# Layer 0's feed-forward stage in seven products per 128 hidden columns, and where the second layer's modulation is computed

## The reference, cut to what matters

```python
cond = jax.nn.silu(c)
for i in range(DEPTH):                       # DEPTH = 2
    mod = (cond @ ada_w[i] + ada_b[i])[:, None, :]
    sh1, sc1, g1, sh2, sc2, g2 = jnp.split(mod, 6, axis=-1)
    h = rmsnorm(x, norm_mix[i]) * (1 + sc1) + sh1
    ...                                      # i = 0: windowed attention, i = 1: dilated attention
    x = x + g1 * y
    h = rmsnorm(x, norm_ffn[i]) * (1 + sc2) + sh2
    x = x + g2 * swiglu(h, ffn_w_in[i], ffn_w_out[i])   # (silu(h@Wg) * (h@Wu)) @ Wo, 2816 hidden columns
```

## Time and profile before

| | us |
|---|---|
| median of 3 runs | 2860.38 (2860.36 to 2861.19) |
| time of the profiled execution | 2857.41 |
| its span in the profile | 2855.6 |
| PE busy | 2738.8 (96%) |
| DVE busy | 1662.7 (58%) |
| ACT busy | 887.2 (31%) |
| POOL busy | 273.4 (10%) |

### The profile page before, as it was taken

The page is one execution under the profiler, slowest core; times in us unless marked ns, Lnnn a source line. Parts: engine busy times, 40 slices in busy tenths (PEclk is TensorE's granted clock), DMA queues, the critical chain, the costliest instruction groups (busy, mean ns, idle before and its releaser), DMA issues. The chain is left out here.

```text
span 2855.6 us, 33976 instructions
## 1 busy us (share of the span) xinstructions
PE 2738.8 (96%) x13022; PEld 2161.8 (76%) x13022; DVE 1662.7 (58%) x2833; ACT 887.2 (31%) x1503; POOL 273.4 (10%) x425
## 2 busy tenths in 40 slices
PE   6999798999999999999998989999999999999798
PEld 5666487888888888876676677888888878879767
DVE  6777745444333334755656688777787785331653
ACT  5544513111111111344444153333333341101132
POOL 2110000000000001100000000000000039920000
PEclk9999899999999999999999899999999999979899
DMA  5223222222222221100011011111111131121212
GB/s 222 82 84 113 106 82 70 84 82 85 91 89 73 73 73 66 74 30 30 23 38 75 30 34 56 51 51 55 51 51 55 48 106 40 51 38 39 81 37 74
DMA packets 145817, 192.55 MB, mean 67 GB/s; under 512 B 6416, under 2 KB 114160, under 8 KB 145424
## 3 DMA queue, kind: packets, MB, share of 16 engines
q1 hardware_dynamic: 133232, 147.44, 15.5%
q0 software_dynamic: 12480, 43.68, 4.9%
HBM read 177.33 MB, written 12.58 MB: 67 GB/s over the span
## 5 line engine op out<-in xcount | busy, mean ns | idle before, releaser
L1101 PE MATMUL psum<-hT_high,w_low 128*128 128x512 f32 x1624 | 469.3, 392 | 2.1 <-DVE arena L2734 2.1
L1101 PEld LDWEIGHTS psum<-hT_high,w_low 128*128 128x128 f32 x1624 | 306.9, 189 | 67.1 <-DVE arena L2734 2.3
L2263 DVE SCALAR_TENSOR_TENSOR xT<-psum,mod,xT 128x1024 f32<-128x1024 f32 x176 | 223.1, 1279 | 72.4 <-PE psum L1385 72.4
L1101 PE MATMUL psum<-hT_high,w_high 128*128 128x512 f32 x744 | 230.3, 391 | 10.7 <-DVE w_low L2533 5.9
L1101 PE MATMUL psum<-h_low,w_high 128*128 128x512 f32 x736 | 227.5, 390 | 0.0
L1148 PE MATMUL psum<-hT_high,w_low 128*128 128x512 f32 x480 | 203.7, 424 | 2.5 <-DVE h_low_mix L2623 1.8
L1864 ACT ACTIVATE arena<-arena 128x384 f32<-128x384 f32 (+3 forms) x320 | 157.6, 494 | 117.1 <-DVE arena L2445 117.1
L1150 PE MATMUL psum<-hT_high,w_low 128*128 128x512 f32 x480 | 188.6, 393 | 0.0
L1149 PE MATMUL psum<-h_low_mix,w_low 128*128 128x512 f32 x480 | 187.7, 391 | 0.0
L2541 DVE TENSOR_TENSOR arena<-arena,psum 128x1024 f32<-128x1024 f32 x22 | 26.9, 1221 | 274.3 <-PE psum L1101 274.3
L1101 PE MATMUL psum<-hid_high,w_low 128*128 128x512 f32 x608 | 183.6, 391 | 0.8 <-DVE hid_low L2643 0.8
(11 more groups left out here) (352 smaller groups left out, 5262.1 us busy)
## 6 DMA issues: line engine op xcount, KB each, us to landing
arena<-in_ada_tiles_dram POOLq DMA_DIRECT2D x48, 512.0 KB, 3.6
wpair<-in_ffn_w_in_dram SPq DMA_DIRECT2D x22, 1024.0 KB, 5.1
wpair<-in_ffn_w_in_dram SPq DMA_DIRECT2D x88, 256.0 KB, 2.9
wpair<-in_ada_tiles_dram POOLq DMA_DIRECT2D x16, 1024.0 KB, 5.3
wpair<-in_w_in_dram SPq DMA_DIRECT2D x24, 512.0 KB, 3.8
wpair<-in_ffn_w_out_dram SPq DMA_DIRECT2D x11, 1024.0 KB, 4.8
wpair<-in_ffn_w_out_dram SPq DMA_DIRECT2D x44, 256.0 KB, 2.8
wpair<-in_b_tiles_dram SPq DMA_DIRECT2D x18, 512.0 KB, 3.3
```

What stands on the lines that cost most here:

```text
L1101: mm = nc.tensor.matmul(dst[:, HALF * t:HALF * t + HALF], w(k), src(k)[:, HALF * t:HALF * t + HALF], start=first and n == 0 and w is high ...
L2263: nc.vector.scalar_tensor_tensor(xT[:, m, :], acc[m % 2] if src is None else src, mod[:, l, 40 + m:41 + m], xT[:, m, :], ALU.mult, ALU.add ...
```

## The change

Layer 0's feed-forward stage is `feed(0, 0)`, the code that layer 1 used before (now `feed(1, 1)`), and `ffn` with its helpers is gone. `norm(1)` makes the first token differences as `norm(3)` does. The memory of the feed stage overlaps `cond`, so silu(c) is loaded and computed a second time (`cond_late`) in the attention of layer 1.

The second layer's 48 modulation tiles go elsewhere: 8 of them with layer 0's in `attention(0, 4)`, where a unit now has five pieces, in steps n = 0, 2, 4, 6 and 7; 8 stay in the `wo` stage (`second_piece`); 32 become `late_piece`, one tile per step in t = 36 to 67, from one landing buffer, issued by POOL when the tile before has been read. SP waits for `ada_read` 20 (16 before) ahead of layer 0's `wo` tiles, and for 60 ahead of layer 1's. In the last step of `feed(0, 0)` SP loads the first two tiles of the next attention, and the first is split there and not in `norm(2)`. POOL's distance and bias tables of layer 1 begin after the last product of the feed stage (before: after the last gate and up tile of `ffn`), and only two of its six bias tables are made ahead.

The diff, cut to its core (the text of the removed `ffn` functions is left out):

```diff
@@ plan_accumulators, plan_weights @@
-    use.block(("ffn", 0), ffn + [0], ffn_frees + [0])
+    use.block(("ffn", 0), [0] * 4, [0] * 4)
...
+    def second_mix(names):
+        for n, name in enumerate(names):
+            s.add(name, (1, 2)[n] if n < 2 else n % 2, name)
...
-    mix(MIX_TILES[1])
+    second_mix(MIX_TILES[1])
@@ buffers @@
+        ada_late, cond_late = wpair[2][:, 0:D], wpair[2][:, D:2 * D]
@@ SP @@
-            sp.wait_ge(ada_read, 16)
+            sp.wait_ge(ada_read, 20)
             for m in range(2, KC):
                 load_tile(("wo", 0, m), wo_rows[0][:, :, P * m:P * m + P], KC)
-            load_ffn(0)
-            load_mix("kv", 4)
+            load_steps(0, lambda n: load_mix(("kv", "q0")[n], 4))
...
+            sp.wait_ge(ada_read, 60)
             for n in range(3):
                 load_tile(("wo", 1, n), wo_rows[1][:, :, 256 * n:256 * n + 256], 4)
@@ POOL @@
-                for k in range(4):
-                    m = 4 * u + k
+                for k in range(5):
+                    m = 5 * u + k
                     if m:
                         pool.wait_ge(ada_read, m)
...
-            with pool.Fori(0, NF // 2) as i:
-                for k in range(KC):
-                    pool.wait_ge(ada_read, 8 * i + (23 + k))
-                    ada_load(bass.ds(8 * i + (8 + k), 1), k)
...
-            pool.wait_ge(ada_read, 16 + 48)
-            d, number = acc_number(("ffn", 0, gate_up_at(NF - 1) + 3))
-            pool.wait_ge(acc_ready[d], number)
+            pool.wait_ge(product_done, product_number(0, STEPS - 1, "P4"))
...
-            for u in range(4, 10):
-                bias_tables(u)
+            bias_tables(4)
+            bias_tables(5)
+            pool.wait_ge(proj_ready[1], bank_use(1, "q01", 4) + 1)
+            pool.dma_start(cond_late, c.to_broadcast([P, D])).then_inc(cond_late_landed, 16)
+            for u in range(4, 8):
+                if u > 4:
+                    bias_tables(u + 1)
+                for k in range(KC):
+                    m = KC * (u - 4) + k
+                    if m:
+                        pool.wait_ge(ada_read, 28 + m)
+                    pool.dma_start(ada_late, ada_tiles[1, 16 + m]).then_inc(ada_landed[0], 16)
+            bias_tables(9)
@@ PE @@
-            ffn(0)
+            feed(0, 0)
...
-            feed(1, 0)
+            feed(1, 1)
@@ ACT @@
+                if first == 4:
+                    act.wait_ge(cond_late_landed, 16)
+                    nc.scalar.activation(cond_late, cond_late, ACT.Silu).then_inc(cond_ready, 1)
...
-            ffn(0)
+            feed(0, lambda: tile_highs(("kv", 4)))
@@ DVE @@
+            def late_piece(m):
+                dve.wait_ge(ada_landed[0], 16 * (m + 5))
+                modulation(ada_late, mod[:, 1, 16 + m:17 + m], vec[:, 64 + m:65 + m], cond_late).then_inc(ada_read, 1)
...
-                tile_lows(("kv", 4))
...
-                if l == 1:
-                    tile_lows(("conv", 0, 0))
+                tile_lows(("conv", 0, 0) if l else ("kv", 4))
...
-                    if t < 32 and n % 2 == 0:
-                        piece(4 * u + n // 2)
+                    if t < 32 and n in (0, 2, 4, 6, 7):
+                        piece(5 * u + (0, 2, 4, 6, 7).index(n))
+                    if t == 36:
+                        dve.wait_ge(cond_ready, 2)
+                    if 36 <= t < 68:
+                        late_piece(t - 36)
...
-            add_modulation(-1, slice(0, 8), slice(48, 56))
-            ffn(0)
+            feed(0, 0)
```

More of the change, by code:

```diff
@@ L125 @@
 CONVS[3:5] = [(1, 0), (0, 3)]
-def gate_up_at(g):
-    return 0 if g == 0 else 4 + 12 * (g - 1)
-def down_at(g):
-    return 8 + 12 * g if g < NF - 1 else 4 + 12 * (NF - 1)
-def is_up(pos):
-    return pos in (2, 3) or pos >= 4 and (pos - 4) % 12 in (2, 3) and pos < down_at(NF - 1)
-def freed_at(pos):
-    return sum(1 for p in range(pos % 3, pos, 3) if not is_up(p))
-TURN = [sum(1 for p in range(4, 28) if p % 3 == d and not is_up(p)) for d in range(3)]
 PIECES = (("kv", 0), ("kv", 1), ("q0", 0), ("q0", 1), ("q1", 0), ("q1", 1))
@@ L189, in plan_accumulators @@
     norm(1)
-    ffn = [len(range(d, 12 * NF, 3)) for d in range(3)]
-    ffn_frees = [freed_at(12 * NF + (d - 12 * NF) % 3) for d in range(3)]
-    use.block(("ffn", 0), ffn + [0], ffn_frees + [0])
+    use.block(("ffn", 0), [0] * 4, [0] * 4)
     norm(2)
@@ L494, in two_blocks_kernel @@
         mixed = sem("mixed")
-        hid_ready = sem("hid_ready")
-        hid_high_ready = sem("hid_high_ready")
-        hid_split = sem("hid_split")
         shifted = sem("shifted")
-        w_high_ready = [sem(f"w_high_ready{s}") for s in range(3)]
-        w_split = [sem(f"w_split{s}") for s in range(3)]
         part_landed = {name: sem(f"part_landed_{name}") for name in RAW}
@@ L1940, in first_weights, with ffn_done @@
[L1940 to L1955 removed]
+            def ffn_done(f, k):
+                act.wait_ge(down_added, KC * (STEPS - 1) + k + (176 * f + 1))
@@ L2120, in copy, with modulation, second_piece @@
                 nc.vector.tensor_copy(dst, a if src is None else src(a)).then_inc(free(name), 1)
-            def modulation(tile, column, start=0.0):
-                return nc.vector.tensor_tensor_reduce(out=tile, in0=tile, in1=cond, scale=1.0, scalar=start, op0=ALU.mult, op1=ALU.add,
+            def modulation(tile, column, start, silu=cond):
+                return nc.vector.tensor_tensor_reduce(out=tile, in0=tile, in1=silu, scale=1.0, scalar=start, op0=ALU.mult, op1=ALU.add,
                                                       accum_out=column)
             def piece(m):
+                l, first = (0, 16 + 2 * m) if m < 16 else (1, 2 * m - 32)
                 dve.wait_ge(ada_landed[2], 16 * (m + 1))
                 for b in range(2):
-                    at = 16 + 2 * m + b
-                    ins = modulation(ada_mid[:, b], mod[:, 0, at:at + 1], vec[:, at:at + 1])
+                    ins = modulation(ada_mid[:, b], mod[:, l, first + b:first + b + 1], vec[:, 48 * l + first + b:48 * l + first + b + 1])
                 ins.then_inc(ada_read, 1)
+            def second_piece(k):
+                dve.wait_ge(ada_landed[k % 2], 16 * (k // 2 + 1))
+                modulation(ada_ffn[k % 2], mod[:, 1, 8 + k:9 + k], vec[:, 56 + k:57 + k]).then_inc(ada_read, 1)
+            def late_piece(m):
+                dve.wait_ge(ada_landed[0], 16 * (m + 5))
+                modulation(ada_late, mod[:, 1, 16 + m:17 + m], vec[:, 64 + m:65 + m], cond_late).then_inc(ada_read, 1)
             def sum_squares(n, k):
```

289 lines of the change are left out of this document (42 added, 247 removed).

## The result

The changed kernel takes 2823.37 us (median of 4 runs, 2822.39 to 2825.33) against 2860.37 for the kernel before beside it. The ratio is 0.9874, with a 95% interval of 0.9857 to 0.9891: 37.0 us or 1.3% faster. Its profiled execution took 2823.84 us with a span of 2821.8; before it was 2857.41 and 2855.6, so the two traces laid over each other have to explain 33.8 us.

What follows compares the result with a forecast made beforehand. PE, busy 96% of the span, was taken as the bound. Terms -46.3 + 2 + 2.1 + 0.8 = -41.4 from 2857.41 gave 2816.0; with the median 3.0 higher, 2819 us, range 2811 to 2834.

Steps and rivals of the forecast that it cites:

- The count of matmuls: Layer 0's feed-forward stage: 2916 matmuls of 512 columns instead of 3168, 252 fewer; PE's ceiling of the gain 57.1 us.
- The stage from its twin: Layer 0's feed-forward stage, read off layer 1's, which already has the new form: 745.7 to 699.4 us, gain 46.3 us.
- Pieces in layer 0's attention: Five pieces per unit instead of four: cost only in unit 3, +2.1 us, bounds 0 and 3.
- The wait at step 31: End of unit 3, layer 0's attention: DVE's normalising waits for step 30's successor piece, starting after 338.0 instead of 336.01, +2.1 us.
- units 0 to 2 hide their extra piece: Layer 0's attention: PE is the bound there and DVE waits, so extra pieces cost nothing; uncovered, 2.4 us each.
- Late tiles: Layer 1's attention, 32 tiles of 1.2 us on DVE, mostly hidden: +0.8 us, bounds 0 and 38.
- The slip in steps n = 1: Layer 1's attention: DVE has no idle time left in four such steps; a late tile costs 0.2 us in each.
- The late landings: Late tiles' transfers issued from GpSimd could wait for descriptors, adding 2.5 to 3.6 us: 7.4 with the read, only just hidden.
- the first rival: Layer 1's attention: late tiles become the bound, one per landing + 1.3 us; landing of 8 us gives about 2878; 4%.
- The silu in unit 4: Start of layer 1's attention: ACT's extra table load and silu fit 3.6 us of room; nothing to 1 us, taken as 0.
- POOL beside DVE: Tail of layer 0's feed-forward stage: POOL's layer 1 tables hold DVE's two-operand operations, +2 us, bounds nothing and 9.
- the seams take more: Rival: DVE held by POOL, n = 1 steps slipping and silu late together; 2833, from 2828 to 2842; 14%.

Runs made afterwards that it cites:

- Experiment 4: Kernel before the change, without the 40 tiles of layer 1's modulation in layer 0's feed-forward stage: 2858.80 us, ratio 0.9996 to the kernel before.
- experiments 1 and 5: Changed kernel, layer 0's 20 attention pieces reset over units 0 to 3: 1, as 5, 6, 5, 4, 2817.17 us; 5, as 6, 7, 7, none, 2807.42 us.

## Why the prediction was right, and where it wasn't

The time (2819 predicted, 2823.4 measured) and the sign came out. By terms:

- **The count of matmuls**: right, 252.
- **The stage from its twin**: 46.3 with 2 taken off for POOL, so 44.3; measured 44.6. Its two halves are off in opposite ways. The tail lost 0.4 us to POOL and not 2, and the head or the seam before it was over a microsecond longer than layer 1's. That the two errors nearly cancel is luck. In the ten executions with the new form the stage took 700.2 to 701.3 us, so its gain is 44.4 to 45.5. Experiment 4 shows that taking PE as the only bound of the old stage was right: 49 us of DVE work less, and 0.1 us.
- **Pieces in layer 0's attention**: the step that failed. The prediction put 2.1 us, all at step 31. Laid over the trace it is 9.2, of which 2.6 come and go without any edit, so the change's own loss is about 6.6. The wait at step 31 is there as described:

```profile
344.79 1.28 DVE L1939 CUSTOM_DVE_ANT_0 wpair<-wpair,arena,vec 128x1024 f32<-128x1024 f32 x1 [2.72 <-DMA wpair<-in_ada_tiles_dram]
```

The normalisation behind it starts 5.8 us after the end of step 31 instead of 2.6, so 3.2 us later where 2.0 were forecast; at the start of the stage only 0.5 of them is left. The sentence that failed is that units 0 to 2 hide their extra piece: they do hide its DVE time, as experiments 1 and 5 show with even more pieces there, but the piece at the end of unit 2 takes the buffer from the first piece of unit 3. I priced every transfer at the 5.3 us of one that ran nearly alone, and didn't lay the new issue times over SP's queue. What would have told it is in the trace of before: x, 4 MB, issued at 279.50. Of DVE's wait of 6.0 us, 3.7 are the load's and 2.3 those of two pieces in neighbouring steps.
- **Late tiles**: 0.8 predicted, 0.36 measured; doubling their transfer costs 50 us, so they are hidden with little to spare. The slip in steps n = 1 is there and recovered, as forecast. The late landings that the prediction drew from the Trainium skill (SBUF — State Buffer; the 620 and 3100 ns stand there in the section A bandwidth-pool intuition that's wrong (but worth ruling out)) aren't seen: the 32 transfers landed in 3.6 us in the median, as before. And where the first rival reaches about 2878 at a landing of 8 us, its own terms give 2880.
- **The silu in unit 4**: 0 predicted. ACT's timeline of the changed kernel:

```profile
1190.66 1.28 ACT L1753 ACT_TABLE_LOAD   x1
1191.96 1.06 ACT L1753 ACTIVATE wpair<-wpair 128x1024 f32<-128x1024 f32 x1
1193.04 1.28 ACT L1732 ACT_TABLE_LOAD   x1
1194.33 0.46 ACT L1732 ACTIVATE arena<-arena 128x192 f32<-128x192 f32 x1
```

From the first load to the end of the second it takes 1193.04 + 1.28 - 1190.66 = 3.66 us, the 3.6 of the sum, with nothing between the three. The dearer switch that the Trainium skill gives (ScalarE: Activation LUTs, What ACT_TABLE_LOAD costs), 2.66 us with its drain, isn't seen: the measured one is 1.30 from start to start.
- **POOL beside DVE**: the Trainium skill's exclusion (SBUF — State Buffer, Who interferes with whom) agrees with the trace on POOL's side: an operation of POOL that begins beside such a one of DVE lasts until that has ended, 1.08 us instead of 0.28. The price is what is left of the other's instruction and not a whole one. On DVE's side the trace doesn't agree, since sums of squares that began during a table operation weren't held; the split was, by 0.27 us, beside a POOL operation of 0.46. What failed in the term is the count and the price, ten operations and four meetings of half a microsecond. Two of DVE's operations were longer, by 0.27 and 0.12 us, and the sums of squares by nothing.

Of the rivals, "the seams take more" was the nearest: 2828 to 2842 by three mishaps at POOL, n = 1 steps and the silu. The loss came from none of these. The time fell inside the range although a term of 6.6 us stood in the sum as 2.1: the term that dominates, the stage, was right, and the range was wide enough for the rest. Added up against the traces, the forecast of 41.4 us less is 7.6 too much: 7.1 in unit 3 and 2.0 at the seams behind layer 1's attention, less 1.4 in three other places (0.7 before unit 3, 0.4 at the late tiles, 0.3 in the stage). By the medians it is only 4.4 too much, because the profiled execution of before lay 3.0 below its median and that of after 0.5 above. The two steps of unit 3 that vary were short in the first and long in the second, which can account for 2.6 of these 3.5. Without them the pieces' term is 4.5 too small, about the whole of the miss by the medians. What is left of the other terms is no larger than what differs between two executions.

## What to carry to other kernels

When a loop over single-buffered transfers is made denser, write down the new issue time of each transfer and lay it over the other queues' issues in the old trace: what counts is not whether DVE has time for the extra work but whether the buffer is free early enough, and who else is moving data then. Put such filler where another engine is the bound; in this kernel a piece of 2.4 us cost nothing beside projections and 1.5 to 2.4 us in the one unit without them, and moving four of them out of it was worth 8 to 10 us, against 45 for the new form of the stage. Where the same kernel has the new form at another place, its twin's length is a good forecast; here it was 1 to 2 us short of 701. And before a loss of a microsecond or two is put down to an edit, run the same kernel again: 2.6 of the 9.2 us here were no edit's.

## What the runs showed of the hardware that I had not expected

- Transfers beside each other were slower each. 1 MB landed in 5.3 us in the median, took 7.4 us beside 512 KB, and 11.1 us beside 4 MB and 512 KB, while the core moved 412 GB/s in all at a DMA share of 1.03.
- After 6 us without a matmul the granted clock was 0.57 in the next 6 us, while the same stretch without the stall had 1.00. Where unit 3 has gaps, five executions of identical code there took 56.0 to 58.8 us and two of the old kernel's code 49.1 and 52.0; without pieces, two took 42.3 and 42.3. In the step that ends with step 28's maxima, the same matmuls kept PE busy for 6.71 us at a granted clock of 0.97 and for 8.03 at 0.82. The low clock needs no stall of 6 us: the kernel of experiment 4 has none there and the longer step. That the clock makes the scatter is likely from these windows, but no run held the clock fixed.
- POOL and DVE, both reading SBUF, met in the tail at a price of 0.4 us for DVE and, in the eight table operations, 1.3 us for POOL. POOL waited for DVE's instruction to end; DVE was held by at most 0.27 us.
